# The tiles of u at a pitch of 520 numbers, its low half 16 bytes and the low weights 64 bytes further on

## The chip, the cores and the metric

One core of one Trainium2 chip runs the whole program. The metric is the device time in microseconds (us) of one execution; lower is better.

## The reference

Two layers (DEPTH = 2) of a block over 256 tokens of x and 256 tokens of a context, 1024 numbers each, in float32. Cut to what matters:

```python
for l in range(DEPTH):
    h  = post_norm(h,  0.5 * mods[2]   * swiglu(modulate(h,  mods[0],   mods[1]),   ffn1_up[l], ffn1_down[l]), ...)
    hc = post_norm(hc, 0.5 * mods_c[2] * swiglu(modulate(hc, mods_c[0], mods_c[1]), ffn1_up[l], ffn1_down[l]), ...)
    y, yc = token_mixer(modulate(h, ...), modulate(hc, ...), ..., w_in[l], ..., w_sc[l], w_ml[l], w_da[l], w_o[l], ...)
    h = post_norm(h, mods[5] * y, ...)
    h = post_norm(h, 0.5 * mods[8] * swiglu(modulate(h, mods[6], mods[7]), ffn2_up[l], ffn2_down[l]), ...)
    # the context takes the last two steps in layer 0 only
```

`swiglu(u, up, down)` is `(silu(a) * v) @ down` with `a, v = split(u @ up)`; up is 1024 x 5632, down 2816 x 1024. `token_mixer` multiplies the modulated h by w_in (1024 x 9232), runs a short convolution, an mLSTM and a differential attention, and joins them by gated products with w_sc, w_ml, w_da and w_o. `u` in the kernel is the modulated h, the input of every up and w_in product.

## The kernel before, in words

Everything lies transposed: features on the 128 partitions, the 512 tokens (256 of the context, then 256 of x) along the free axis. h and u are 8 tiles of 128 x 512 each (KD = 8, TOK = 512). In layer 1 the context falls away after the keys and values of the mixer, and most products run on the 256 tokens of x alone, from column 256 on (`t0 = 256`).

**Float32 in three products.** Each operand a is kept as a high half a_hi (float32r) and a low half a_lo = a - a_hi (float32r). A product is w_hi a_hi + w_hi a_lo + w_lo a_hi. The activations u, g (the hidden layer of swiglu), z and the y's exist as such pairs. The weights are cut on the fly: a chunk of weights (128 x 1024 numbers, up to 8 blocks of 128 x 128) is brought by SP's DMA into one of 2 slots of `raw` (in the last part of layer 1 also 2 slots in h), ScalarE copies it to a slot of w_hi (line 1015), VectorE subtracts to make w_lo (line 1341); w_hi and w_lo have 4 slots (SPLIT).

**The chunk** is what TensorE repeats 512 times (lines 658 to 672). For one output tile of 128 features it runs over the k blocks and issues three matmuls for each:

```python
pe.matmul(ps[bank][:, t0:TOK], wh, a_hi, start=a, stop=False)      # line 669
pe.matmul(ps[bank][:, t0:TOK], wh, a_lo, start=False, stop=False)  # line 670
m = pe.matmul(ps[bank][:, t0:TOK], wl, a_hi, start=False, stop=b)  # line 671
```

The weights are the stationary operand: each matmul has a weight load of its own, 128 x 128, which runs beside the matmul before it. The activation is the moving operand, 512 or 256 columns. Lines 684 to 686 are the same three matmuls at the start of a stage, where four chunks go side by side through k as the tiles of u come (`interleaved`); line 798 is the same for the 16 gate columns of w_in, whose split weights are wg_hi and wg_lo. Line 652 (`ada_chunk`) computes the modulation vectors: there w_hi and w_lo are the moving operand and a 4-column block of `cs_parts` the stationary one.

**The order of work** is written out by hand for each engine; semaphores join them. Per layer: up (22 x 2 tiles), down (8 tiles), norm, mixer with proj (48 chunks), gates and w_o, norm, up, down, norm. In the norms ScalarE writes u_hi (line 1063) and VectorE u_lo (line 1451), tile by tile.

**Where things lie** (bytes in a partition). The helper `at` hands out places one behind the other from byte 16512 on, in steps of 32 bytes; `region`, 96 KB for g, z, the y's and the like, comes after the small tables. From the code: before the change h starts at 16512, u_hi at 32896, u_lo at 49280, raw at 65664, w_hi at 73856, w_lo at 90240, region (and g_hi) at 117792. So every tile of u_hi and u_lo and every slot of raw, w_hi and w_lo starts 128 bytes behind a multiple of 2048; the blocks of 128 x 128 weights lie 512 bytes apart. The tiles of g, z and the y's, and wg_hi and wg_lo, start 1056 bytes behind a multiple of 2048 (wg's blocks 512 bytes apart). Counted modulo 64, u and the weights start at 0, and g, z, y and wg at 32.

Of the kernel before, what the change touches and what calls it, by code (L numbers as in the profile page):

```python
# [17 lines left out]
F32R = mybir.dt.float32r  # L18
# [4 lines left out]
P = 128  # L23
D = 1024
KD = D // P
SEG = 256
TOK = 2 * SEG
# [201 lines left out]
def build(nc, x, c, ctx, c_ctx, w_ada, b_ada, ln_g, ln_b, ffn1_up, ffn1_down, ffn2_up, ffn2_down,  # L229
          w_in, b_in, conv_w, w_sc, w_ml, w_da, w_o, lam_q1, lam_k1, lam_q2, lam_k2, da_norm_g,  # L230
          consts, out):
    spot = [16512]

    def at(name, shape, dtype, offset=None):

        size = int(np.prod(shape[1:])) * 4
        if offset is None:
            offset = spot[0]
            spot[0] += (size + 31) // 32 * 32
        return nc.alloc_sbuf_tensor_at(name, shape, dtype, offset=offset)  # L240

    h = at("h", [P, KD, TOK], F32)
    u_hi = at("u_hi", [P, KD, TOK], F32R)
    u_lo = at("u_lo", [P, KD, TOK], F32R)
    raw = at("raw", [P, RAW, D], F32)
    w_hi = at("w_hi", [P, SPLIT, D], F32R)
    w_lo = at("w_lo", [P, SPLIT, D], F32R)
    con = at("con", [P, 1154], F32)
    ada_sum = con[0:4, 1152:1154]
# [92 lines left out]
    ps = [nc.alloc_psum_tensor(f"ps{i}", [P, 512], F32) for i in range(8)]  # L342
# [260 lines left out]
    def _(pe):  # L603
# [28 lines left out]
        for b in range(4):  # L632
            pe.wait_ge(stage_in[b], 64)
            for k in range(KD):
                m = pe.matmul(ps[4 + b][0:2, :], cs[:, k, :], stage[:, 4 * b + k // 2, (k % 2) * BLOCK:(k % 2 + 1) * BLOCK],
                              start=(k == 0), stop=(k == KD - 1))
# [156 lines left out]
        def gates(layer):  # L793

            pe.wait_ge(wg_ready, layer + 1)
            for k in range(KD):
                for n, (w, a) in enumerate(((wg_hi, u_hi), (wg_hi, u_lo), (wg_lo, u_hi))):
                    m = pe.matmul(ps[6][:, :], w[:, k, :], a[:, k, :], start=(n == 0 and k == 0),
                                  stop=(n == 2 and k == KD - 1))
            m.then_inc(mg_done, 1)  # L800

# [112 lines left out]
        def mixer(layer):  # L914
            t0 = t0_of(layer)
            pe.wait_ge(evac_dve, BASES[layer, "proj"][2])
            for step in ORDERS[layer]:
                if step[0] in EVAC_ENGINE:
                    proj(layer, step)
                elif step[0] == "ada":  # L920
                    r = BASES[layer, "proj"][0] + PLANS[layer][step][0]
                    ada_chunk(r, r % SPLIT, ADA_OF[layer, "proj"] + step[1], step[2])
                elif step[0] == "adat":
                    ada_columns(ADA_OF[layer, "proj"] + step[1])
                elif step[0] == "attend":
                    attend(layer)
                elif step == ("gates", 0):
                    gates(layer)
                elif step[0] == "ml_gates":
                    gates_turn(layer)  # L930
                elif step[0] == "ml_t":
                    turn_h(layer, step[1], TT - 1)
                elif step[0] in ("ml_s", "ml_n"):
                    (ml_scores if step[0] == "ml_s" else ml_numerator)(layer, *step[1:])
                elif step[0] in ("turn_v", "rope"):
                    {"turn_v": turn_v, "rope": rope}[step[0]](layer, step[1])
# [54 lines left out]
        for q in range(2):  # L991
            pe.wait_ge(h_ready, KD * 6 + 4 * (q + 1))
            for s in range(2):
                n = 2 * q + s
                for k in range(4):
                    m = pe.transpose(ps[n][:, k * P:(k + 1) * P], h[:, 4 * q + k, SEG + s * P:SEG + (s + 1) * P], ident)
# [906 lines left out]
```

## Time and profile before

| what | value |
|---|---|
| median of the runs | 2742.84 us (2 runs, 2741.74 and 2743.94) |
| span of the profiled execution | 2748.9 us |
| TensorE matmul busy | 2614.5 us, 95% |
| VectorE busy | 1436.4 us, 52% |
| ScalarE busy | 1139.1 us, 41% |
| DMA | 320.18 MB, mean 116 GB/s |
| mean granted TensorE clock | 0.984 of 2.4 GHz |

The profiled execution gives one time, its span; it stands 6.1 us (0.2%) above the median of the runs. Matmuls overlap: the duration of one includes its way through the array, so their rate is read from the distance of their starts in the timeline, not from the durations. A difference of two durations of the same width is a difference of that distance.

### The profile page before, as it was taken

Reading aid. Unit: us, or ns where it says so; the run is one execution under the profiler, and the core shown is the slowest. Engines: PE = TensorE matmul, PEld = TensorE weight load, DVE = VectorE, ACT = ScalarE, POOL = GpSimd, SP = SyncE. Lnnn points to the kernel's source line nnn. Section 1 sums busy time; section 2 is a strip of 40 time slices with the busy share of each in tenths; the row PEclk is TensorE's granted clock in tenths of the full one; section 3 lists DMA queues with packets and bytes.
Section 4 is the critical chain, followed back from the end, with each engine's and each line's share of the span. In section 5 each row is a group of like instructions: output and inputs, shape, how many; then the busy total and the mean of one; then the engine's idle time right before and its main releaser. Section 6 shows DMA issues by size and latency. Waiting matters only on the chain.

```text
span 2748.9 us, 36856 instructions
## 1 busy us (share of the span) xinstructions
PE 2614.5 (95%) x12940; PEld 2094.7 (76%) x12940; DVE 1436.4 (52%) x2179; ACT 1139.1 (41%) x1598; POOL 0.2 (0%) x4
## 2 busy tenths in 40 slices
PE   7999999899999799998999998999998999898998
PEld 3777777577777577775777776888886888698998
DVE  3444454565446744455444545333446565667565
ACT  3334433443353543325344334332225353555545
POOL 0000000000000000000000000000000000000000
PEclk9999999899999999999999999999999999999999
DMA  6455544253222044432555532333232343165554
GB/s 215 131 159 160 151 129 137 66 154 107 62 62 66 8 123 123 122 113 67 153 157 156 145 104 73 99 99 95 81 99 77 107 108 96 54 183 157 168 166 125
DMA packets 519453, 320.18 MB, mean 116 GB/s; under 512 B 13974, under 2 KB 481344, under 8 KB 519360
## 3 DMA queue, kind: packets, MB, share of 16 engines
q1 hardware_dynamic: 517912, 318.59, 40.6%
q8 instruction: 56, 0.92, 0.1%
q10 hardware_dynamic: 1448, 0.38, 0.1%
q14 instruction: 37, 0.30, 0.0%
HBM read 317.87 MB, written 1.05 MB: 116 GB/s over the span
## 4 chain that ended last, share of the span: by engine, by line
PE 79%; DVE 8%; ACT 5%; DMA 5%; issue 2%; SPq 1%; ACTq 0%; DVEq 0%
PE ps L669 22%; PE ps L671 22%; PE ps L670 21%; PE ps L652 3%; ACT w_hi L1015 2%; DVE w_lo L1341 2%; DMA raw<-in_ffn_down 2%; PE ps L854 2%; DMA raw<-in_w_ada 2%; PE ps L754 2%; PE ps L684 1%; PE ps L685 1%; PE ps L686 1%; PE ps L626 1%; DMA raw<-in_ffn_up 1%
## 5 line engine op out<-in xcount | busy, mean ns | idle before, releaser
L1341 DVE TENSOR_TENSOR w_lo<-raw,w_hi 128x1024 fp32r<-128x1024 f32 x574 | 702.8, 1225 | 963.8 <-ACT w_hi L1015 958.2
L1015 ACT ACTIVATE w_hi<-raw 128x1024 fp32r<-128x1024 f32 x574 | 607.4, 1059 | 1174.8 <-PE ps L671 665.5
L669 PE MATMUL ps<-u_hi,w_hi 128*128 128x512 f32 (+1 forms) x2368 | 863.0, 364 | 10.5 <-DVE w_lo L1341 5.4
L670 PE MATMUL ps<-u_lo,w_hi 128*128 128x512 f32 (+1 forms) x2368 | 850.5, 359 | 0.0
L671 PE MATMUL ps<-u_hi,w_lo 128*128 128x512 f32 (+1 forms) x2368 | 850.2, 359 | 0.0
L669 PEld LDWEIGHTS ps<-u_hi,w_hi 128*128 128x128 f32 x2368 | 449.4, 190 | 88.2 <-DVE w_lo L1341 14.0
L671 PEld LDWEIGHTS ps<-u_hi,w_lo 128*128 128x128 f32 x2368 | 449.2, 190 | 67.0
L670 PEld LDWEIGHTS ps<-u_lo,w_hi 128*128 128x128 f32 x2368 | 449.4, 190 | 65.6 <-issue 1.0
L669 PE MATMUL ps<-g_hi,w_hi 128*128 128x512 f32 (+1 forms) x704 | 259.6, 369 | 0.0
L671 PE MATMUL ps<-g_hi,w_lo 128*128 128x512 f32 (+1 forms) x704 | 259.3, 368 | 0.0
L670 PE MATMUL ps<-g_lo,w_hi 128*128 128x512 f32 (+1 forms) x704 | 259.0, 368 | 0.0
L669 PEld LDWEIGHTS ps<-g_hi,w_hi 128*128 128x128 f32 x704 | 132.9, 189 | 26.1
L670 PEld LDWEIGHTS ps<-g_lo,w_hi 128*128 128x128 f32 x704 | 133.0, 189 | 24.1
L671 PEld LDWEIGHTS ps<-g_hi,w_lo 128*128 128x128 f32 x704 | 132.7, 189 | 24.2
L1107 ACT ACTIVATE g_hi<-scr 128x512 f32 (+3 forms) x88 | 50.9, 578 | 174.6 <-DVE scr L1513 143.6
L684 PE MATMUL ps<-u_hi,w_hi 128*128 128x512 f32 (+1 forms) x192 | 74.1, 386 | 36.8 <-DVE u_lo L1451 36.8
L652 PE MATMUL ps<-w_hi,cs_parts 128*4 128x512 f32 x256 | 101.4, 396 | 0.0
L652 PE MATMUL ps<-w_lo,cs_parts 128*4 128x512 f32 x256 | 100.4, 392 | 0.0
L1341 DVE TENSOR_TENSOR w_lo<-h,w_hi 128x1024 fp32r<-128x1024 f32 x66 | 80.5, 1224 | 33.9 <-ACT w_hi L1015 32.2
L1516 DVE TENSOR_TENSOR g_lo<-scr,g_hi 128x512 f32 (+3 forms) x88 | 55.1, 626 | 76.2 <-ACT g_hi L1107 76.2
L1015 ACT ACTIVATE w_hi<-h 128x1024 fp32r<-128x1024 f32 x66 | 69.6, 1055 | 43.1 <-PE ps L671 43.0
L684 PEld LDWEIGHTS ps<-u_hi,w_hi 128*128 128x128 f32 x192 | 40.1, 209 | 46.4 <-issue 39.8
(237 smaller groups left out, 2574.2 us busy)
## 6 DMA issues: line engine op xcount, KB each, us to landing
raw<-in_ffn_up SPq DMA_DIRECT2D x154, 512.0 KB, 3.8
raw<-in_w_in SPq DMA_DIRECT2D x132, 512.0 KB, 3.8
raw<-in_w_ada SPq DMA_DIRECT2D x128, 512.0 KB, 3.8
raw<-in_ffn_down SPq DMA_DIRECT2D x64, 384.0 KB, 3.5
raw<-in_ffn_down SPq DMA_DIRECT2D x48, 320.0 KB, 3.2
h<-in_ffn_up SPq DMA_DIRECT2D x22, 512.0 KB, 3.9
stage<-in_w_ada SPq DMA_DIRECT2D x16, 512.0 KB, 11.2
raw<-in_w_ml SPq DMA_DIRECT2D x12, 512.0 KB, 3.9
```

Source lines behind the costliest of these rows:

```text
L626: m = pe.matmul(ps[bank][:, 2 * t:2 * t + 2], ada_row[0:rows_n, t * P:(t + 1) * P], pick, start=True, stop=True)
L652: m = pe.matmul(ps[4][0:4, :], stationary, part[:, slot, e * BLOCK:(e + 1) * BLOCK], start=(j == 0 and e == 0 and part is w_hi), stop=(j = ...
L669: pe.matmul(ps[bank][:, t0:TOK], wh, a_hi, start=a, stop=False)
L670: pe.matmul(ps[bank][:, t0:TOK], wh, a_lo, start=False, stop=False)
L671: m = pe.matmul(ps[bank][:, t0:TOK], wl, a_hi, start=False, stop=b)
L684: pe.matmul(ps[q][:, t0:TOK], wh, u_hi[:, k, t0:TOK], start=(k == 0), stop=False)
L754: pe.matmul(ps[7][:, t0:TOK], mean_w, scr[k % 2][:, t0:TOK], start=(k == 0), stop=(k == KD - 1)).then_inc(ln_sq_used, 1)
L854: m = pe.matmul(ps[6 + n][:, 0:257], pw[:, n, s, t * P:(t + 1) * P], vaug[:, s, head, :], start=(s == keys[0]), stop=(s == keys[-1]))
L1015: act.activation(split_tiles(w_hi, slot), raw_tiles(raw_slot), ACT.Copy).then_inc(hi_done, 1)
L1107: act.activation(g_hi[:, 2 * i + q // 2, t0:TOK], scr[2 + q // 2][:, t0:TOK], ACT.Copy).then_inc(g_hi_done, 1)
L1341: dve.tensor_tensor(split_tiles(w_lo, slot), raw_tiles(place[0]), split_tiles(w_hi, slot).bitcast(F32), ALU.subtract).then_inc(lo_done, 1)
L1516: dve.tensor_tensor(g_lo[:, 2 * i + e, t0:TOK], scr[2 + e][:, t0:TOK], g_hi[:, 2 * i + e, t0:TOK].bitcast(F32), ALU.subtract).then_inc(g_r ...
```

## The change

Only addresses change. No instruction is added, removed or moved on any engine.

```diff
     h = at("h", [P, KD, TOK], F32)
-    u_hi = at("u_hi", [P, KD, TOK], F32R)
-    u_lo = at("u_lo", [P, KD, TOK], F32R)
+    u_hi = at("u_hi", [P, KD, TOK + 8], F32R)
+    u_lo = at("u_lo", [P, KD * (TOK + 8) + 8], F32R)[:, 4:4 + KD * (TOK + 8)].rearrange("p (k n) -> p k n", k=KD)
+    spot[0] += 96
     raw = at("raw", [P, RAW, D], F32)
     w_hi = at("w_hi", [P, SPLIT, D], F32R)
+    spot[0] += 64
     w_lo = at("w_lo", [P, SPLIT, D], F32R)
...
-                    m = pe.matmul(ps[6][:, :], w[:, k, :], a[:, k, :], start=(n == 0 and k == 0),
+                    m = pe.matmul(ps[6][:, :], w[:, k, :], a[:, k, 0:TOK], start=(n == 0 and k == 0),
```

The last line only leaves out the 8 unused numbers behind each tile. From the code, the places afterwards:

| tensor | before | after | start modulo 64 before | after |
|---|---|---|---|---|
| u_hi, tile k | 32896 + 2048k | 32896 + 2080k | 0 | 0 for even k, 32 for odd k |
| u_lo, tile k | 49280 + 2048k | 49552 + 2080k | 0 | 16 for even k, 48 for odd k |
| raw | 65664 | 66304 | 0 | 0 |
| w_hi | 73856 | 74496 | 0 | 0 |
| w_lo | 90240 | 90944 | 0 | 0 |
| g_hi (region) | 117792 | 118496 | 32 | 32 |

Modulo 128, w_lo lay with w_hi at 0 and afterwards lies at 64; g lay at 32 and afterwards lies at 96.

## Rows read from the trace of the kernel before

**Rows 1.** The page: busy time, and the chain that ended last.
```profile
PE 2614.5 (95%) x12940; PEld 2094.7 (76%) x12940; DVE 1436.4 (52%) x2179; ACT 1139.1 (41%) x1598; POOL 0.2 (0%) x4
...
PE 79%; DVE 8%; ACT 5%; DMA 5%; issue 2%; SPq 1%; ACTq 0%; DVEq 0%
```

**Rows 2.** The waits of PE: us in total, times, longest us.
```profile
PE ps L684 <- DVE u_lo L1451: 36.8, 8, 7.2
...
PE ps L669 <- DVE w_lo L1341: 5.4, 3, 2.6
```

**Rows 3.** Groups with shapes apart: count | busy us, mean ns of one | idle before.
```profile
L670 PE MATMUL ps<-u_lo,w_hi 128*128 128x512 f32 x1664 | 650.4, 391 | 0.0
...
L670 PE MATMUL ps<-g_lo,w_hi 128*128 128x512 f32 x528 | 209.7, 397 | 0.0
...
L670 PE MATMUL ps<-u_lo,w_hi 128*128 128x256 f32 x704 | 200.1, 284 | 0.0
...
L685 PE MATMUL ps<-u_lo,w_hi 128*128 128x512 f32 x128 | 53.0, 414 | 0.0
...
L670 PE MATMUL ps<-g_lo,w_hi 128*128 128x256 f32 x176 | 49.2, 280 | 0.0
...
L685 PE MATMUL ps<-u_lo,w_hi 128*128 128x256 f32 x64 | 19.6, 307 | 0.0
...
L798 PE MATMUL ps<-u_lo,wg_hi 128*128 128x512 f32 x16 | 6.4, 399 | 0.0
L798 PE MATMUL ps<-u_hi,wg_hi 128*128 128x512 f32 x16 | 6.3, 394 | 0.0
L798 PE MATMUL ps<-u_hi,wg_lo 128*128 128x512 f32 x16 | 6.3, 392 | 0.0
```

**Rows 4.** Timeline of PE, up of layer 0, u of 512 columns: start, us.
```profile
299.83 0.39 PE L669 MATMUL ps<-u_hi,w_hi 128*128 128x512 f32 x1
300.05 0.39 PE L670 MATMUL ps<-u_lo,w_hi 128*128 128x512 f32 x1
...
303.00 0.39 PE L671 MATMUL ps<-u_hi,w_lo 128*128 128x512 f32 x1
```

**Rows 5.** Timeline of PE, down of layer 0, g of 512 columns.
```profile
454.99 0.39 PE L670 MATMUL ps<-g_lo,w_hi 128*128 128x512 f32 x1
...
458.03 0.40 PE L671 MATMUL ps<-g_hi,w_lo 128*128 128x512 f32 x1
```

**Rows 6.** Timeline of PE, last up, u of 256 columns.
```profile
2599.74 0.28 PE L670 MATMUL ps<-u_lo,w_hi 128*128 128x256 f32 x1
...
2601.18 0.28 PE L670 MATMUL ps<-u_lo,w_hi 128*128 128x256 f32 x1
```

**Rows 7.** Timeline of PE, last down, g of 256 columns.
```profile
2711.78 0.28 PE L670 MATMUL ps<-g_lo,w_hi 128*128 128x256 f32 x1
...
2713.66 0.28 PE L671 MATMUL ps<-g_hi,w_lo 128*128 128x256 f32 x1
```

**Rows 8.** Line 670 from 2562 to 2700 us: duration ns min/median/max.
```profile
L670 PEld LDWEIGHTS ps<-u_lo,w_hi x294: 192/192/192, 2561.8 to 2667.3; 128*128 128x128 f32 x147
L670 PE MATMUL ps<-u_lo,w_hi x294: 283/283/283, 2561.9 to 2667.4; 128*128 128x256 f32 x147
...
L670 PE MATMUL ps<-g_lo,w_hi x92: 277/280/282, 2667.8 to 2699.8; 128*128 128x256 f32 x92
```

**Rows 9.** Timeline of PE, the mLSTM numerators, 257 columns of plain float32.
```profile
691.03 3.20 PE L854 MATMUL ps<-vaug,pw 128*128 128x257 f32 x14
694.06 0.38 PE L840 MATMUL ps<-con,hs 128*128 128x128 f32 x2
```

**Rows 10.** Line 652, weights as moving operand: duration ns min/median/max.
```profile
L652 PEld LDWEIGHTS ps<-w_hi,cs_parts x256: 82/85/88, 85.6 to 1586.0; 128*4 128x4 f32 x128
L652 PE MATMUL ps<-w_hi,cs_parts x256: 387/397/472, 85.8 to 1586.2; 128*4 128x512 f32 x128
```

**Rows 11.** Windows: us, busy PE, PEld, DVE, ACT, POOL, granted clock, DMA share, GB/s.
```profile
299.00:304.00 5.00, 5.00 (x24) 3.71 (x23) 2.48 (x4) 2.18 (x3) 0.00 (x0) 1.00 0.52 129
...
2555.00:2700.00 145.00, 145.00 (x1217) 145.00 (x1216) 89.39 (x112) 74.48 (x101) 0.00 (x0) 1.00 0.62 181
```

**Rows 12.** Groups with shapes apart: the instructions that write u.
```profile
L1063 ACT ACTIVATE u_hi<-h,mod_b,mod_a 128x256 fp32r<-128x256 f32 x88 | 47.4, 587 | 24.4 <-DVE h L1436 19.4 <-DVEq L1430 4.9
...
L1451 DVE TENSOR_TENSOR u_lo<-scr,u_hi 128x512 fp32r<-128x512 f32 x40 | 27.7, 693 | 3.7 <-ACT u_hi L1063 2.5
```

**Rows 13.** DMA issues of the page: count, KB each, us to landing.
```profile
raw<-in_ffn_up SPq DMA_DIRECT2D x154, 512.0 KB, 3.8
```

## The prediction

> **What bounds the kernel now.** I read the busy table and the chain first [rows 1]: PE holds 95% of the span and 79% of the chain that ended last, VectorE is at 52% and ScalarE at 41%. Then the waits of PE [rows 2]: the longest in total is for u_lo at the start of the stages, 36.8 us in 8 waits, and PE waits for split weights 5.4 us in all. So the time is the number of matmuls times the distance at which they follow one another, and a change of addresses counts if it alters this distance. The transfers do not bind: in the middle of an up stage the DMA share is 0.52, in the last up stage, where a chunk is shortest, 0.62, with PE busy throughout at a granted clock of 1.00 (2.4 GHz) [rows 11]; a chunk lands in 3.8 us [rows 13], with more than one slot in flight.
>
> Next I took the distance itself from the timeline. In up, with u of 512 columns, starts at 299.83 and 303.00 lie 14 matmuls apart: 226.4 ns each [rows 4]. In down, with g, 454.99 and 458.03 lie 13 apart: 233.8 ns [rows 5]. With 256 columns, u takes 1.44 us for 12, 120.0 ns [rows 6], and g 1.88 us for 16, 117.5 ns [rows 7]. At one column per cycle of 2.4 GHz the columns need 213.3 and 106.7 ns. So u pays 13.1 and 13.3 ns over its columns, the same for both widths; g pays 20.5 and 10.8 ns, growing with the width. The two stages use the same split weights, banks of the same kind and the same lines; what differs is where the moving tiles start: at 0 modulo 64 bytes for u, as the weights do, and at 32 for g. The gate columns confirm it from the other side: there u is the moving operand and the weights, wg, start at 32 modulo 64, and the durations are 394, 399 and 392 ns instead of some 389 [rows 3, 4]. A duration stands about 163 ns above the distance (283 against 120 in rows 6 and 8), so these are distances of 231, 236 and 229. The addresses of both operands thus set the distance already in the kernel before, by up to 10 ns of 226.
>
> The matmuls at issue are those with u as moving operand. 512 columns: 1664 in each of the three lines of the chunk, 128 in each of the three lines of the interleaved start, 16 in each of three groups for the gates, 5424 in all [rows 3]. 256 columns: 704 and 64 in three lines each, 2304 [rows 3]. Together 7728. With g there are 3 x 528 and 3 x 176.
>
> **The change part by part.**
>
> *Pitch of 520 and 16 bytes for u_lo.* In before, each matmul on u begins at the same place modulo 64 as the one ahead. Afterwards the three matmuls of a block go hi, lo, hi, so the start moves by +16, -16 and then +32 bytes to the next k. No row of before has such a step between one moving tile and the next, so the price is bounded from both sides.
>
> The best end: plain float32, which takes two cycles a column, shows nearly no cost between matmuls. Fourteen of 257 columns stand in 3.20 us; the next instruction starts 3.03 us after the first [rows 9], 216.4 ns each, against 214.2 for 514 cycles, so some 2.3 ns. If all matmuls on u came down to that, each would save about 10.9 ns: 7728 x 10.9 = 84 us.
>
> The worst end: u at the largest duration of a whole group, 399 against 389 ns [rows 3, 4], costs 10 ns on 5424 matmuls, 54 us; nearer at hand is g's behaviour: +7.4 ns x 5424 = 40 us, and -2.5 ns x 2304 = -6 us, together +34 us.
>
> The value that I take lies between. u's cost does not depend on the width, so I read it as a wait at the start, for a point in a pattern that turns with the address; g, half of 64 bytes off the weights, falls into no fixed step. If 13.3 ns is a whole number of turns and a turn is 64 bytes of the stream (16 columns, 6.7 ns; this length is an assumption, half of 13.3), u waits for the second turn each time. A step of the address by 16, 48 or 32 bytes then moves the meeting point by 1.7, 5.0 or 3.3 ns: waits of 8.3, 11.7 and 10.0 ns in place of 13.3, on average 3.3 ns less. That is near what the trace has at its shortest: the least duration with 512 float32r columns in these rows is 387 ns, 2 under u's 389 [rows 4, 10], and g of 256 columns has 277 at least and 280 in the median where u has 283 throughout [rows 8]. 3.3 ns x 7728 = 25.5 us.
>
> *The weights' 64 bytes and the shift of g.* Modulo 64 nothing changes for w_hi, w_lo and g, so I take 0 for 1584 and 528 matmuls. Were a longer pattern at work, g could win or lose what u and g differ by: 7.4 ns x 1584, 12 us either way. Weight loads play a part: beside u of 256 columns all take 192 ns [rows 8], but even with a weight load of 4 columns, 85 ns, the matmul of line 652 keeps a median of 397 [rows 10]. So it is not the volume of the load that costs, and I give the 64 bytes no gain of their own.
>
> *The rest.* ScalarE's 88 wide writes of u_hi (587 ns) and VectorE's 40 of u_lo (693 ns) [rows 12] go to other addresses. They are on the path where PE waits 36.8 us at the starts of stages; if they altered by 1% it would be under 1 us. I take 0. The line of the gates drops nothing that costs.
>
> **A rule of the Trainium skill.** The rows show 226.4 ns at one address and 233.8 at another [rows 4, 5]. The Trainium skill (TensorE: Matmul & The Clock Gate, section "Wait — 56ns, not 53.3ns?") has back-to-back warm matmuls at N/2.4 + 2.5 ns, so 216 for 512 columns whatever the address, and the Trainium skill (SBUF — State Buffer, section "Who interferes with whom") says that PE never waits on anyone. By these the addresses could not matter and the change would do nothing. The trace disagrees with the first by 10 and 18 ns; the second leaves open whether PE's two reads disturb each other.
>
> **The sum.** 25.5 us from u. Where PE is fed late the gain is lost for a while; with PE at 95% busy I keep nine tenths, 23 us. Against the span of 2748.9 that is 2726; the runs stand 6.1 us lower (2742.84), so 2720, a gain of 0.8%. Both ends, in the same way: -84 us gives about 2660, +34 gives 2777.
>
> **The rivals.**
>
> *Slower: the fixed step is lost.* u's tiles and the weights lie alike modulo 64, and this is what keeps all matmuls on u in one regular step of 226 ns. With u at 0, 16, 32 and 48 the step is broken, and u behaves like g and like the gates: 234 at 512 columns, 117.5 at 256. Place: every up and proj chunk. Price: +34 us, 2777. It decides from the point where the average distance on 512 columns is above about 228 ns. For it: every pair of unlike addresses in the trace is slower at 512 columns [rows 3, 5]. Against it: at 256 columns the unlike pair is the faster [rows 6, 7], and within g the address never steps from tile to tile, so g does not show what a step does.
>
> *Nothing measurable: a wait of the same length elsewhere.* The distance may be set by the weight load and its own address, which modulo 64 does not change; then u wins at 256 what it loses at 512, or neither. Time within 8 us of 2743. For it: line 652, with moving tiles placed like u's and other stationary addresses, spreads from 387 to 397 in minimum and median [rows 10]. Against it: u and g differ with the same w_hi.
>
> *Much faster: the steps fit the pattern and the wait goes.* The start of each matmul then falls where the stream ahead ends, at some 2.3 ns as plain float32 shows [rows 9]: -84 us, about 2660. Halfway, -8 ns, gives 2683. For it: steps of 16 and 32 bytes are 1.7 and 3.3 ns of stream, of the size of that gap. Against it: no float32r matmul in the rows at 512 columns comes under 387 ns, that is 224.
>
> **How the numbers follow.** Forecast (a few ns per matmul on u, 2700 to 2733): 0.38. Nothing measurable: 0.18. Slower, 2752 to 2785: 0.20. Much faster, 2655 to 2700: 0.24. The range from 2668 to 2778 takes in the slower case and most of the large gain. A measurement of this kernel can tell about 2% from no change, 55 us: only the larger part of the last case lies beyond it (0.22); slower by over 2% needs u at the worst group of the trace throughout, 0.04; the rest is 0.74.
>
> **What would show it.** In the profile after, the mean of the groups of u at 512 columns (391 now) should be near 388 and at 256 columns (284) near 281, those of g unchanged at 397 and 280, and the three lines no longer alike, since the step ahead of each differs. The number of instructions, the waits and the DMA shares should stay. The forecast is wrong if u's groups go to 397 or more (the fixed step lost), or to 380 and less (the wait gone), or if g's groups move though its place modulo 64 has not; in that last case the pattern is longer than 64 bytes.

## The result, and the profile after

The changed kernel takes 2760.0 us (2 runs, 2759.42 and 2760.58), the kernel before 2742.84: the ratio is 1.0059, with a 95% interval of 1.0038 to 1.0080. So it is slower by some 17 us, where I had forecast 23 us faster; the time lies in the range, on the other side of the kernel before. The interval excludes 1, so the loss is clear of noise, though it is far below 2%.

The page of the kernel after, busy time and chain, against [rows 1]:

```profile
span 2757.7 us, 36856 instructions
...
PE 2628.1 (95%) x12940; PEld 2088.6 (76%) x12940; DVE 1436.5 (52%) x2179; ACT 1139.0 (41%) x1598; POOL 0.2 (0%) x4
...
PE 81%; DVE 7%; ACT 5%; DMA 4%; issue 2%; SPq 0%; ACTq 0%; DVEq 0%
```

PE is busy 13.6 us longer; VectorE and ScalarE are where they were (1436.5 and 1139.0), and so is the count of instructions. The waits of PE don't carry the loss: the longest in total is as in [rows 2], and the one for w_lo fell from 5.4 to 3.2 us.

```profile
PE ps L686 <- DVE u_lo L1453: 37.0, 9, 7.2
...
PE ps L671 <- DVE w_lo L1343: 3.2, 2, 1.9
```

(The changed kernel has two more lines ahead of this code, so line 671 is 669 of before, 686 is 684, and so on.) The groups with shapes apart, count | busy us, mean ns of one, against [rows 3]:

```profile
L671 PE MATMUL ps<-u_hi,w_hi 128*128 128x512 f32 x1664 | 666.7, 401 | 6.3 <-DVE w_lo L1343 3.2 <-ACT scr L1106 3.1
L673 PE MATMUL ps<-u_hi,w_lo 128*128 128x512 f32 x1664 | 656.9, 395 | 0.0
L672 PE MATMUL ps<-u_lo,w_hi 128*128 128x512 f32 x1664 | 655.2, 394 | 0.0
...
L672 PE MATMUL ps<-g_lo,w_hi 128*128 128x512 f32 x528 | 208.7, 395 | 0.0
...
L672 PE MATMUL ps<-u_lo,w_hi 128*128 128x256 f32 x704 | 198.3, 282 | 0.0
```

u of 512 columns went from 391 to 394 ns in u_lo's line, and in total over the three lines of the chunk from 1960.3 us (659.9, 650.4 and 650.0) to 1978.8: 18.5 us more. u of 256 columns fell from 284 to 282. And g, whose place modulo 64 is what it was, fell from 397 to 395. That is the sign that my prediction named for a pattern longer than 64 bytes.

The distance of starts, from the timeline of PE at the place of [rows 4]:

```profile
300.15 0.40 PE L672 MATMUL ps<-u_lo,w_hi 128*128 128x512 f32 x1
300.38 0.39 PE L673 MATMUL ps<-u_hi,w_lo 128*128 128x512 f32 x1
...
303.63 0.40 PE L672 MATMUL ps<-u_lo,w_hi 128*128 128x512 f32 x1
```

15 matmuls in 3.48 us are 232.0 ns each, against 226.4. That the step is also no longer regular shows in the least, median and largest duration over one stretch. Line 670 of before from 300 to 440 us, and the same line after:

```profile
L670 PE MATMUL ps<-u_lo,w_hi x61: 389/389/397, 300.1 to 349.6; 128*128 128x512 f32 x61
```

```profile
L672 PE MATMUL ps<-u_lo,w_hi x64: 387/393/399, 300.1 to 352.5; 128*128 128x512 f32 x64
```

**The distances in all kernels.** From here on a distance is the mean over all pairs of neighbouring starts in one trace, at full clock and under 260 ns apart (so without the waits), averaged over the three kinds of step (hi to lo, lo to hi, and on to the next block). "Sum" multiplies the differences to before by the counts of the prediction, 5424, 2304, 1584 and 528. "Measured" is the ratio of the runs less one, times 2743 us. A group's mean duration is a blunter measure: it holds the matmuls at the lower clock too, so over all of u at 512 columns it rose by 3.7 ns where the distance rose by 4.6.

| kernel | u 512 | u 256 | g 512 | g 256 | sum, us | measured, us |
|---|---|---|---|---|---|---|
| before | 227.4 | 120.3 | 234.1 | 117.3 | | |
| the change | 232.0 | 119.5 | 232.0 | 117.8 | +19.8 | +16 |
| pitch alone (e1_pitch) | 232.6 | 118.6 | 234.1 | 117.3 | +24.3 | +20 |
| u_lo alone (e2_lo16) | 231.1 | 118.5 | 234.2 | 118.7 | +16.6 | +9 |
| w_lo alone (e3_wlo64) | 231.1 | 118.4 | 231.2 | 117.8 | +11.3 | +10 |
| weights 32 bytes on (e5_swap) | 233.2 | 118.8 | 226.9 | 120.0 | +17.7 | +15 |
| region 96 bytes on (e4_again; e4_region0 alike) | 227.4 | 120.4 | 227.0 | 120.0 | -9.9 | -5 and -7 |
| halves 128 bytes further apart (c1_alike) | 232.1 | 118.5 | 232.4 | 117.8 | +18.6 | +15 |
| alike modulo 256, tiles of 256 columns 112 bytes on (c2_alike) | 227.7 | 115.1 | 227.0 | 113.3 | -24.1 | -17 |

The sum has the sign of the measurement everywhere; between half and nine tenths of it arrives. (It does not order the two smallest losses: u_lo alone has 16.6 and w_lo alone 11.3, and the runs, +9 and +10, cannot tell them apart.)

A large part of what does not arrive is the granted clock. Span times mean granted clock, averaged over the runs, counts a run in time at full speed; it is an estimate, good to 1 or 2 us, from clocks with three decimals. It falls by 23.1 us for c2_alike (sum 24.1), whose five runs have a mean clock of 0.9822 against 0.9847, and by 10.8 and 10.0 us for e4_region0 and e4_again (sum 9.9; 0.9827 and 0.9835 against 0.9849 and 0.9847). For u_lo alone it rises by 13.8 us (sum 16.6), at a mean clock of 0.9867 against 0.9849. So the faster kernels pay part of their gain back at the lower clock, and this slower one gets part of its loss back. For w_lo alone this does not close the sum: 7.7 us of 11.3.

The theories that the runs were to tell apart: *the pair of addresses sets the distance* (u and the weights alike: one regular step, all else slower at 512 columns), against *a wait of the same length whatever the addresses*, *the other engines disturb PE's reads*, and my own forecast.

### The profile page after: what moved, and what is told of

Its sections match the earlier page's. It is cut to its first block, busy times and chain, and to the rows that moved or that the text cites. A ratio compares the mean times of both kernels' runs of the same rounds, so it can differ in the third digit from the quotient of the medians.

```text
span 2757.7 us, 36856 instructions
## 1 busy us (share of the span) xinstructions
PE 2628.1 (95%) x12940; PEld 2088.6 (76%) x12940; DVE 1436.5 (52%) x2179; ACT 1139.0 (41%) x1598; POOL 0.2 (0%) x4
## 4 chain that ended last, share of the span: by engine, by line
PE 81%; DVE 7%; ACT 5%; DMA 4%; issue 2%; SPq 0%; ACTq 0%; DVEq 0%
PE ps L671 22%; PE ps L673 22%; PE ps L672 22%; PE ps L654 3%; ACT w_hi L1017 2%; DMA raw<-in_ffn_down 2%; DVE w_lo L1343 2%; PE ps L856 2%; PE ps L756 2%; DMA raw<-in_w_ada 2%; PE ps L686 1%; PE ps L687 1%; PE ps L688 1%; PE ps L628 1%; PE ps L637 1%
```

## The experiments

### One part of the change at a time

The pitch of 520 alone (u_hi and u_lo both start as before, and so do the weights and g, modulo 256):

```diff
-    u_hi = at("u_hi", [P, KD, TOK], F32R)
-    u_lo = at("u_lo", [P, KD, TOK], F32R)
+    u_hi = at("u_hi", [P, KD, TOK + 8], F32R)
+    u_lo = at("u_lo", [P, KD, TOK + 8], F32R)
```

> Only the pitch of u_hi and u_lo is 520; every start modulo 128 of the rest stays as before, and tile k of both halves starts at 32k. Theory A (the regular step of 226 ns on u needs moving tiles and weights that start alike modulo 64 bytes): the odd tiles break it, u's 512-column groups go from a mean of 391 to 393 to 396 ns, total +8 to +20 us. Theory B (it is w_lo's 64 bytes that cost, the pattern being 128 bytes long): u's groups stay at 391, total 0 +-3 us. g unchanged at 397 in both.

Measured: 2765.32 us against 2744.1, 1.0074 (1.0060 to 1.0088). The groups of u and g:

```profile
L670 PE MATMUL ps<-u_lo,w_hi 128*128 128x512 f32 x1664 | 656.4, 394 | 0.0
...
L670 PE MATMUL ps<-g_lo,w_hi 128*128 128x512 f32 x528 | 210.2, 398 | 0.0
```

u is at 394, g stays at 398. The pitch alone costs about as much as the whole change; the two intervals overlap.

The 16 bytes of u_lo alone:

```diff
-    u_lo = at("u_lo", [P, KD, TOK], F32R)
+    u_lo = at("u_lo", [P, KD * TOK + 8], F32R)[:, 4:4 + KD * TOK].rearrange("p (k n) -> p k n", k=KD)
+    spot[0] += 96
```

> Only u_lo starts 16 bytes further on. Theory A: every second change of operand breaks the step, u's 512-column groups at 393 to 397 ns, total +8 to +25 us. Theory B: 391, 0 +-3 us. g unchanged at 397 in both.

Measured: 2752.74 us, 1.0032 (1.0020 to 1.0044). u of 512 columns at 231.1 ns. This run is not as clean as it was meant to be: the room of u_lo and the 96 bytes behind it move raw, w_hi, w_lo and g by 128 bytes, and only later did a run show that 128 bytes are not nothing. The bare series below, matmuls with nothing beside them, has u_lo's 16 bytes with nothing else: 231.8.

The 64 bytes of w_lo alone:

```diff
     w_hi = at("w_hi", [P, SPLIT, D], F32R)
+    spot[0] += 64
     w_lo = at("w_lo", [P, SPLIT, D], F32R)
+    spot[0] += 64
```

> Only w_lo starts 64 bytes further on (region stays at the same place modulo 128). Theory A (64 bytes is the length of the pattern): nothing moves, u 391, g 397, total 0 +-3 us. Theory B (128 bytes): u's groups go to 394 to 397 and the total to +10 to +20 us, or g's groups move by 2 ns as they did in the changed kernel (397 to 395).

Measured: 2754.24 us, 1.0038 (1.0024 to 1.0052). I had given this part nothing.

```profile
L673 PE MATMUL ps<-u_hi,w_lo 128*128 128x512 f32 x1664 | 660.8, 397 | 0.0
...
L672 PE MATMUL ps<-u_lo,w_hi 128*128 128x512 f32 x1664 | 653.0, 392 | 0.0
...
L672 PE MATMUL ps<-g_lo,w_hi 128*128 128x512 f32 x528 | 207.8, 393 | 0.0
```

The line that loads w_lo is the slowest now (397; 391 before), and the two others, whose addresses are as before, lose 1 to 2 ns in distance. g goes from 397 to 393: here the region moved by 128 bytes too. So each part costs, and together they cost no more than the pitch alone. That the prices do not add up fits a regular step that is lost once, but the step can be lost for more or for less: the bare series below run from 228.4 to 235.6.

### Giving g what u had, and taking it from u

If the pair of addresses decides, g (at 32 modulo 64, the weights at 0) can be given u's step by moving the region by 96 bytes, to the place of u modulo 256:

```diff
+    spot[0] += 96
     region = spot[0]
     spot[0] += 96 * 1024
```

> Only region (g, z, the y's, wg) starts 96 bytes further on, so that its tiles start at 0 modulo 128 as the weights do. Theory A: g, z, y and the gates get u's regular step: g's 512-column groups 397 to 390, the gates' 392 to 399 to about 389, g at 256 columns 280 to 283; total -10 to -14 us (7.4 ns on 2160 matmuls, less 2.5 on 1104). Rival C (what is special about u is its own place or its stage, not that it lies like the weights): g stays at 397, total 0 +-3 us.

> The same kernel as e4_region0, for a comparison beside c1_alike. Ratio 0.996 to 0.9995; 12 us of matmul distance are saved, of which half were lost to waits in the down stages before.

Measured: 2738.22 us against 2744.1, 0.9980 (0.9971 to 0.9989), and again 2735.61 against 2741.99, 0.9976 (0.9967 to 0.9985). Both are faster than the kernel before, by less than the 10 to 14 us expected. The groups of the second:

```profile
L671 PE MATMUL ps<-u_lo,w_hi 128*128 128x512 f32 x1664 | 649.9, 391 | 0.0
...
L671 PE MATMUL ps<-g_lo,w_hi 128*128 128x512 f32 x528 | 207.3, 393 | 0.0
```

g's distance goes from 234.1 to 227.0, u's stays. g's mean duration is 393, where 389 is its median, because more of its matmuls run at half the clock: 8 of g at 512 columns started there before, 20 in this run and 29 in the first of the two. One such place is a down stage of layer 0. At the same point PE waited 0.55 us for `ada_row` before and waits 0.94 us now, and a few matmuls later the granted clock (the column after POOL's) falls to 0.50, where the kernel before kept 1.00:

```profile
463.40 1.05 PE L626 MATMUL ps<-con,ada_row 4*128 4x2 f32 x8 [0.55 <-DVE ada_row L1362]
...
464.80:468.00 3.20, 3.20 (x16) 2.56 (x15) 2.51 (x4) 1.69 (x2) 0.00 (x0) 1.00 0.22 65
```

```profile
461.70 1.05 PE L627 MATMUL ps<-con,ada_row 4*128 4x2 f32 x8 [0.94 <-DVE ada_row L1363]
...
463.70:466.80 3.10, 3.10 (x8) 2.35 (x8) 3.07 (x5) 1.06 (x1) 0.00 (x0) 0.50 0.27 81
```

Each of the 12 or 21 more matmuls is 200 ns dearer there (427 against 227), 2.4 or 4.2 us, of the size of what the sum lacks. A faster g comes earlier to a result that VectorE has not finished; that this longer wait brings the clock down is likely from the order of events, but no run varied the wait alone.

The mirror image moves the weights by 32 bytes, to the place of g, and leaves u (the 96 bytes behind take the region 128 bytes on, so that g and the weights are alike modulo 256):

```diff
     raw = at("raw", [P, RAW, D], F32)
+    spot[0] += 32
     w_hi = at("w_hi", [P, SPLIT, D], F32R)
     w_lo = at("w_lo", [P, SPLIT, D], F32R)
+    spot[0] += 96
```

> Only w_hi and w_lo start 32 bytes further on (region stays as it was modulo 128), so that now g, z and y lie like the weights, and u does not. Theory A (what counts is the pair): u's and g's 512-column distances change places, by p1_phases u to 233.3 and g to 226.7: +6.4 ns x 5424 - 7 ns x 2160 = +19 us, range +12 to +25, ratio 1.0045 to 1.009. Rival C (u's place is good by itself): u stays at 227, total 0 +-3 us.

Measured: 2757.09 us against 2741.99, 1.0056 (1.0042 to 1.0070).

```profile
L672 PE MATMUL ps<-u_lo,w_hi 128*128 128x512 f32 x1664 | 658.9, 396 | 0.0
L671 PE MATMUL ps<-g_hi,w_hi 128*128 128x512 f32 x528 | 208.1, 394 | 0.0
L672 PE MATMUL ps<-g_lo,w_hi 128*128 128x512 f32 x528 | 207.6, 393 | 0.0
```

u and g have changed places: u at 233.2, g at 226.9, and at 256 columns u at 118.8 and g at 120.0. So the distance goes with where the two operands lie to each other, and not with the place of one alone.

### The matmuls alone

Four kernels hold nothing but series of float32r matmuls in the form of the chunk, 4 to 8 turns over 8 blocks with three matmuls each, with no other engine at work beside them. Their output is not that of the layers, and their times are no comparison. Weights and moving tiles start at chosen places; "0" stands for the place of u and the weights in the kernel before (128 modulo 256 bytes).

```python
m = [pe.matmul(b, W(wh, k), M(mh, k)), pe.matmul(b, W(wh, k), M(ml, k)), pe.matmul(b, W(wl, k), M(mh, k))][-1]
```

> A kernel of its own: nothing but series of 96 float32r matmuls (hi, lo, hi over 8 blocks of weights), no other engine at work; the output is a copy of the last sums and not the layers' result. All moving tiles of a series start at m, all weights at w modulo 128 bytes, m and w in steps of 16; pitch 512. Theory A (alike modulo 128 gives the regular step; first 64, by e3_wlo64 128 bytes): mean duration about 389 to 390 ns on the 8 series with m = w, 392 to 400 on the others; at 256 columns with w = 0: 283 at m = 0, 280 to 281 at m = 32. Rival D (neither address matters by itself, the distance comes from what the other engines do in SBUF): all series alike, at 379 to 383 ns, near 216 ns apart.

Measured (1556.35 us): the mean distance at 512 columns, after the first turn of each series, w_hi and w_lo together in the rows, u_hi and u_lo together in the columns, in steps of 16 bytes:

```
w \ u    0      16     32     48     64     80     96    112
  0    226.7  231.6  233.3  233.4  228.9  231.1  233.3  231.2
 16    233.3  233.3  226.7  232.3  231.9  226.7  230.1  233.3
 32    233.3  233.3  226.7  231.6  233.3  233.4  228.8  231.1
 48    233.3  226.7  226.7  230.0  228.4  232.3  231.9  226.7
 64    233.4  234.6  233.4  226.7  226.7  231.6  233.3  233.4
 80    232.0  228.9  233.3  226.7  226.7  230.0  228.4  232.3
 96    234.3  233.3  233.4  234.6  233.4  226.7  226.7  231.6
112    233.3  226.7  232.0  228.9  233.3  226.7  226.7  230.0
```

Sixteen of the 64 pairs have 226.7, which is the least; none is below. The others lie between 228.4 and 234.6. So the spread needs no VectorE, no ScalarE and no DMA, and the rival of the other engines is out. The expectation was only half right on which pairs are good: of the eight on the diagonal, where all starts are alike, four have 226.7 (at 0, 32, 64 and 96) and four have 230.0 or 233.3; and twelve pairs off it have 226.7 too. "Alike" is thus no rule, only a choice that works at multiples of 32.

> The same bare series with the low half of the moving tiles at ml and the low weights at wl modulo 128 (in steps of 16), the high ones at 0; and the layouts of before, of the change and of its three parts. Theory A: before's layout 389 to 390 ns, the change and each part 392 to 397, in the order of the kernels (pitch worst); at 256 columns the change below before by 1 ns. No layout clearly under 387. Rival E (some staggered layout takes the wait away): at least one series at 384 ns or less.

Measured (1772.83 us): the parts of the change one by one, on the same matmuls, as the durations (least/median/largest) and the first and last start of each series. In this order: as before; pitch 520; u_lo 16 bytes on; w_lo 64 bytes on; all three.

```profile
L57 PE MATMUL ps<-act_in,wts x96: 389/389/797, 37.3 to 61.0; 128*128 128x512 f32 x96
...
L59 PE MATMUL ps<-act_in,wts x96: 387/394/400, 61.3 to 83.3; 128*128 128x512 f32 x96
...
L61 PE MATMUL ps<-act_in,wts x96: 387/396/402, 83.6 to 105.6; 128*128 128x512 f32 x96
...
L63 PE MATMUL ps<-act_in,wts x96: 388/392/398, 105.8 to 127.8; 128*128 128x512 f32 x96
...
L65 PE MATMUL ps<-act_in,wts x96: 388/393/400, 128.0 to 150.0; 128*128 128x512 f32 x96
```

Their distances are 226.7, 232.5, 231.8, 231.0 and 232.0 (the last: from 128.0 to 150.0, 95 steps, 231.6 as far as one decimal tells). The kernels had 232.6, 231.1, 231.1 and 232.0. This comes near the answer to the whole question in five rows: the addresses alone give the loss of each part to within a nanosecond. For the pitch and for w_lo the series has the kernel's places modulo 256 exactly. For u_lo and for the whole change it leaves out 128 bytes by which the kernels' weights had moved too (see below), so that the last 232.0 equals the kernel's is not proof that the same mixture is at work. Of the 64 pairs of a u_lo and a w_lo moved in steps of 16 bytes, with u_hi and w_hi at 0, only two keep 226.7: (0, 0) and (48, 112). The rest have 228.9 to 235.6.

> The bare series at 256 columns, 192 matmuls each; output again a copy of the last sums. First all 64 pairs of m (moving) and w (weights) modulo 128, then single shifts from m = 112, w = 0, then 128 and 384 columns. In p1_phases 256 columns stood at 120.0 ns apart for m = w = 0 and at 113.3 for m = 112, w = 0. Theory A (only the pair counts, steps of the distance are caused by the phase of the two streams): other pairs at 113.3 too, at about the same difference m - w; 120.0 at m = w. Rival F (113.3 came from the state in which the series ahead left the engine): here m = 112, w = 0 stands at 118 to 120.

Measured (2229.83 us), 256 columns: the pairs now lie between 113.3 and 123.3. The one of the kernel before, 120.0 with a median duration of 283 ns, is none of the good ones, and one with u 112 bytes further has 113.3 and 275:

```profile
L57 PE MATMUL ps<-act_in,wts x192: 278/283/582, 37.1 to 62.2; 128*128 128x256 f32 x192
```

```profile
L71 PE MATMUL ps<-act_in,wts x192: 275/275/278, 198.1 to 219.8; 128*128 128x256 f32 x192
```

One pair does not keep to one distance. With u 64 bytes further, the same instructions on the same places stand 113.3 ns apart here, all 192 of them, and 117.8 ns apart in p1_phases and in p4_far. The row from here, then the one from p4_far:

```profile
L65 PE MATMUL ps<-act_in,wts x192: 276/276/276, 130.3 to 151.9; 128*128 128x256 f32 x192
```

```profile
L167 PE MATMUL ps<-act_in,wts x144: 279/279/280, 1496.4 to 1513.2; 128*128 128x256 f32 x144
```

So for this pair something of rival F holds: something besides the addresses, such as the state in which the matmuls ahead left PE, picks among more than one steady step. The three series also ran on three different chips, so the chip is not excluded.

> The bare series once more (output a copy of the last sums), now with shifts in steps of 128 bytes up to 2048: of both halves of the moving tile together, of its low half alone, of the low weights alone, and of the pitch, at 512 columns; at 256 columns both halves together from 0, 64 and 112. c1_alike, which put 128 bytes between u_hi and u_lo and 256 before the weights, lost u's 226.7 ns (232). Theory A with a pattern of 128 bytes: all shifts here are without effect, 226.7 throughout, and c1_alike's loss has another cause. Theory A2 (the pattern is longer, 256, 512 or 1024 bytes): shifts that are multiples of its length give 226.7, the others 229 to 235; since the blocks of weights lie 512 bytes apart and u keeps its step over them, 512 at most is the likeliest.

Measured (1918.98 us): how far the pattern reaches. u_hi and u_lo together at 0, 128, 256 and 384, then w_lo alone at 0, 128 and 256:

```profile
L57 PE MATMUL ps<-act_in,wts x144: 387/389/796, 37.2 to 72.6; 128*128 128x512 f32 x144
...
L59 PE MATMUL ps<-act_in,wts x144: 387/394/398, 72.9 to 106.2; 128*128 128x512 f32 x144
...
L61 PE MATMUL ps<-act_in,wts x144: 389/389/395, 106.5 to 138.9; 128*128 128x512 f32 x144
...
L63 PE MATMUL ps<-act_in,wts x144: 387/394/398, 139.1 to 172.5; 128*128 128x512 f32 x144
...
L101 PE MATMUL ps<-act_in,wts x144: 389/389/389, 763.5 to 795.9; 128*128 128x512 f32 x144
...
L103 PE MATMUL ps<-act_in,wts x144: 389/396/397, 796.1 to 829.1; 128*128 128x512 f32 x144
...
L105 PE MATMUL ps<-act_in,wts x144: 389/389/389, 829.4 to 861.8; 128*128 128x512 f32 x144
```

From 72.9 to 106.5 us are 144 steps of 233.3, from 106.5 to 139.1 144 of 226.4. All shifts by a multiple of 256, up to 2048, gave 226.7, and all by an odd multiple of 128 gave 233.4 (u together), 228.9 (u_lo alone) or 231.1 (w_lo alone). In these series the pattern is 256 bytes long. A pitch of 512 + 64 numbers, 256 bytes more, keeps 226.7; 512 + 32 has 232.2. The change holds a step that I did not see at all: with the 128 bytes (modulo 256) that u_lo's shift and the 96 behind it take, w_hi went from 128 to 0 modulo 256, while u_hi's first tile stayed at 128. No run has this step in the change's own layout by itself.

### Kernels built on it

With the first numbers for 256 columns (113.3 at 112 bytes) I moved u and g by 28 numbers where tiles of 256 columns are read, with hi and lo as tensors of their own and room for the shift behind each, which puts 128 more bytes between them; the region moved as above:

```diff
-    g_hi = at("g_hi", [P, KF, TOK], F32R, region)
-    g_lo = at("g_lo", [P, KF, TOK], F32R, region + KF * TOK * 4)
+    g_hi_all = at("g_hi", [P, KF * TOK + 32], F32R, region)
+    g_lo_all = at("g_lo", [P, KF * TOK + 32], F32R, region + KF * TOK * 4 + 128)
```

> e4_region0, and in layer 1 the tiles that only serve 256 columns (u after the mixer and u of the mixer, g of the last down) start 112 bytes further on, where p1_phases has 113.3 ns in place of 120.0. Theory A: 2304 + 528 matmuls of 256 columns at 113.3 to 115, the 480 of 512 columns on u of the mixer at 231 in place of 226.7: -6 ns x 2832 + 4 ns x 480 = -15 us below e4_region0, ratio to before 0.990 to 0.995. Rival G (in the kernel the series is interrupted too often, or the supply of weights sets the pace at 2.8 us a chunk): the distance stays at 118 to 120 or waits take the gain, ratio 0.996 to 0.999.

Measured: 2754.96 us against 2741.99, 1.0054 (1.0040 to 1.0067): a miss. The 128 bytes were taken for harmless, since all series up to then had been laid out within 128 bytes. It is this miss that led to the series on 128 and 256 bytes above. Those explain it in part only. Modulo 256 its u of 512 columns lies, outside the shifted stretches, as in the series with u_lo alone at 128, which has 228.9; in the kernel 15 matmuls take 3.50 us, 233.3 each:

```profile
301.19 0.40 PE L681 MATMUL ps<-u_hi,w_hi 128*128 128x512 f32 x1
...
304.69 0.40 PE L681 MATMUL ps<-u_hi,w_hi 128*128 128x512 f32 x1
```

This is a second case of one set of places with two distances, now at 512 columns.

The same idea with every spacing a multiple of 256: u_hi and u_lo in one tensor, g_hi and g_lo in another, the halves 16 KB and 44 KB apart as before, and only the view moved.

```diff
+    def view(whole, tiles, half, shift):
+        first = half * tiles * TOK + shift
+        return whole[:, first:first + tiles * TOK].rearrange("p (k n) -> p k n", k=tiles)
+
+    def u_of(n):
+        return tuple(view(u_all, KD, half, 28 if n >= 4 else 0) for half in range(2))
...
+    def g_of(layer, f):
+        return tuple(view(g_all, KF, half, 28 if t0_of(layer) and f else 0) for half in range(2))
```

> This is the arrangement of the two runs of the region 96 bytes further on (all starts alike modulo 256 bytes), with one more edit that keeps every spacing a multiple of 256 where it was one: in the layer of 256 columns a tile (norms from the fourth on) u lies 112 bytes further inside its room, and so does g in the last down. Theory (the distance of two matmuls is set by the two addresses modulo 256): u and g of 256 columns come down from 120 to between 113.3 and 115 ns over some 2304 and 528 matmuls, u of 512 columns stays at 227.4 and g of 512 at 227, save the 480 of 512 columns that also read the shifted u, which go to some 231. That is 17 us less than the region alone gave, 0.990 to 0.995 of the time before, some 2720 us. Rival (the weights' supply and the other engines take what the matmuls give): the distances come down as said and the time stays at 0.996 to 0.999. Second rival (something else than these addresses decides): the distances of 256 columns stay at 120, and the time at 0.998.

Measured: 2728.34 us against 2745.10 (5 and 9 runs), 0.9939 (0.9926 to 0.9953). It beats the kernel before and the change. PE's matmuls are the same 12940; besides addresses only 40 instructions more differ, 36896 in all. Its busy time and groups, where u and g are now one tile each:

```profile
PE 2590.6 (95%) x12940; PEld 2083.3 (76%) x12940; DVE 1436.1 (53%) x2179; ACT 1139.9 (42%) x1598; POOL 0.2 (0%) x4
...
L681 PE MATMUL ps<-g,w_hi 128*128 128x512 f32 x528 | 207.5, 393 | 0.0
...
L681 PE MATMUL ps<-u,w_hi 128*128 128x256 f32 x704 | 195.5, 278 | 0.0
```

and the last stages, from 2555 to 2695 us, against [rows 8], for the line that takes the low half: every one of 272 records on u and 140 on g is 275 ns long, where it was 283 and a spread around 280.

```profile
L681 PE MATMUL ps<-u,w_hi x272: 275/275/275, 2555.0 to 2647.1; 128*128 128x256 f32 x136
...
L681 PE MATMUL ps<-g,w_hi x140: 275/275/275, 2647.5 to 2694.7; 128*128 128x256 f32 x140
```

PE's busy time is 23.9 us lower than before's (2614.5), and the sum of the table is 24.1. The runs show 17, 7 us less. Part of the difference in busy time is the profiled execution of before, which stood 6.1 us above its median; the sum at full clock does not depend on that, and its 7 us match the lower granted clock said above (0.9822 against 0.9847).

## Why the prediction was wrong

*What bounds the kernel.* Right in the main: number of matmuls times distance gives the sign in every run and half to nine tenths of the size. The nine tenths that the sum kept for late feeding had no row behind it; what the runs show in its place is, for a good part, a granted clock that falls when the kernel gets faster.

*That the addresses of both operands change the distance.* Right: the exchange of u and g and the bare series show it. That they alone fix it is not: two sets of places had two distances each (113.3 and 117.8; 228.9 and 233.3). The rival "nothing measurable" (the step set by the weight load alone) falls by the bare series too: with w at 0, moving u alone goes from 226.7 to 233.4.

*The failed step: "a step of the address by 16, 48 or 32 bytes then moves the meeting point by 1.7, 5.0 or 3.3 ns", so 3.3 ns less on average.* Measured: 4.6 ns more on 5424 matmuls (+25 us) and 0.8 ns less on 2304 (-2 us). I took u's 13.3 ns for a wait which any other meeting point would shorten. At 512 columns none shorter was found: over 64 pairs of one shift, 64 of two, and twelve pitches, nothing came below 226.66. The regular step of the kernel before was the best, not the worst. Only at 256 columns was there room beneath, and there the change found little of it. The unit that was assumed fits several steady steps: 226.66 and 120.00 with all addresses alike, the best one, 113.33, and 173.3 measured for 384 columns are 34, 18, 17 and 26 times 6.67 ns, 16 columns. Others, such as 117.8, are no such multiple, so this stays a fit and not a shown mechanism. (A small slip in the rivals: 8 ns on 7728 matmuls is 62 us, so halfway is 2681 and not 2683.)

*The second failed step: "modulo 64 nothing changes for w_hi, w_lo and g, so I take 0".* In the bare series the pattern is 256 bytes long. w_lo's 64 bytes alone cost 3.7 ns per matmul on u at 512 columns, and the kernel took 1.0038 of the time; and g of 512 columns, which the change moved by 64 bytes against w_hi modulo 256 (w_hi went from 128 to 0, g from 32 to 224), gained 2.1 ns, 3 us, within the 12 us that I had allowed either way.

*The rival that was right: "Slower: the fixed step is lost".* The loss of the regular step, its place and its condition (above about 228 ns) are what happened; its price was +34 us, of which half came. It took u to g's 234; measured was 232.0, where u's tiles now lie at many places and g's at one. I had it at 0.20, below the forecast at 0.38. What should have raised it stood in the rows: both kinds of unlike pairs at 512 columns were slower [rows 3, 5], and not one was faster. I had set against it the 256 columns [rows 6, 7], which are a different case, and the least duration of 387 in line 652 [rows 10], one matmul of a spread that is wide on both sides.

*The two rules that were cited.* By the Trainium skill (TensorE: Matmul & The Clock Gate, section "Wait — 56ns, not 53.3ns?"), 512 columns stand 216 ns apart. No run here shows that for float32r: the least was 226.66. The Trainium skill (SBUF — State Buffer, section "Who interferes with whom") says that PE never waits on anyone. The bare series agree as far as the other engines go: the layout of before gives 226.7 without them and 227.4 among them. That the places of PE's own operands matter lies outside that rule.

*What stays open.* Why 256 bytes, and what inside PE makes the distance longer. What picks among two steady steps on the same places. What the sum lacks beyond the granted clock, for w_lo alone above all. And whether a pair exists at 512 columns below 226.66: only steps of 16 bytes with few combinations were tried.

## What to carry to other kernels

Where PE is busy throughout, read the distance of matmul starts for each operand and width before touching anything else: a median that equals the least and the largest (389/389/389) is a regular step, and a spread (387/394/400) is a lost one. A regular step need not be the shortest: 283/283/283 at 256 columns is 6.7 ns above the best. No staggered layout beat the aligned one at 512 columns here. What kept the step was the start of every tile at one place modulo 256 bytes, a multiple of 32, with all spacings multiples of 256; count the padding, which moves everything behind it. Measure the addresses in a bare series first, for each width apart, and then in the kernel, since the two can differ (228.9 and 233.3 on the same places).

## What the runs showed that was not expected

A float32r matmul's distance at full clock depends on the places of both operands modulo 256 bytes, though not on them alone: the series spread from 226.7 to 235.6 ns at 512 columns and from 113.3 to 123.3 at 256. In the stretches seen at the lower clock there is nothing of it. The kernel before, 104 to 106 us, at a granted clock of 0.50 (1.2 GHz; the column after POOL's), a microsecond after the end of a wait of 1.86 us for w_lo:

```profile
104.00:106.50 2.50, 2.50 (x8) 1.94 (x7) 1.15 (x1) 0.53 (x2) 0.00 (x0) 0.50 0.57 203
```

```profile
104.31 0.63 PE L669 MATMUL ps<-u_hi,w_hi 128*128 128x512 f32 x1
...
106.02 0.63 PE L670 MATMUL ps<-u_lo,w_hi 128*128 128x512 f32 x1
```

Four steps in 1.71 us are 427 ns, and 512 columns at 1.2 GHz are 426.7. These are u and the weights, alike. g, which at full clock stands 234 ns apart, has the same four steps in 1.71 us there, again in the kernel before:

```profile
428.23 0.63 PE L669 MATMUL ps<-g_hi,w_hi 128*128 128x512 f32 x1
...
429.94 0.63 PE L670 MATMUL ps<-g_lo,w_hi 128*128 128x512 f32 x1
```

What costs 13 to 21 ns over the columns at full speed does not show at half of it.

A matmul of 256 columns in the best place, 113.3 ns, pays 6.7 ns over its columns, where one of 512 pays at least 13.3. By these numbers, as an estimate, two matmuls of 256 columns are no dearer than one of 512; no run put one in place of the other.
